# A two-layer decoder trunk: the first blocks of each MLP's down weights loaded earlier, and two small groups of work reordered

## The reference

```python
D_MODEL, SEQ, DEPTH, D_FF = 1024, 512, 2, 4096

def squared_relu_mlp(h, w_up, w_down):
    a = jax.nn.relu(h @ w_up)
    return (a * a) @ w_down

for layer in range(DEPTH):
    g = norm_gains[layer]
    hn = rmsnorm(x, g[0])
    ...                       # mix = attention of this layer on hn
    x = x + rmsnorm(mix, g[1])
    hn = rmsnorm(x, g[2])
    x = x + rmsnorm(squared_relu_mlp(hn, w_mlp_up[layer], w_mlp_down[layer]), g[3])
```

## Time and profile before

| | before |
|---|---|
| median of three executions | 1149.12 us (1147.21 to 1149.67) |
| the profiled execution's own time | 1146.72 us |
| its span | 1144.9 us |
| PE busy | 1085.0 us, 95% |
| DVE busy | 743.2 us, 65% |
| ACT busy | 541.0 us, 47% |
| POOL busy | 192.9 us, 17% |
| mean granted TensorE clock | 0.98 of full |

### The profile page before, as it was taken

How to read it: one execution, slowest core, us unless ns; L and a number is a source line. 1 busy time by engine, 2 the same in 40 slices (tenths; PEclk the granted TensorE clock), 3 DMA queues, 4 the chain that set the end, 5 groups by cost and what they waited for, 6 DMA issues and landing times. The chain is left out here.

```text
span 1144.9 us, 14901 instructions
## 1 busy us (share of the span) xinstructions
PE 1085.0 (95%) x5433; PEld 870.5 (76%) x5433; DVE 743.2 (65%) x1284; ACT 541.0 (47%) x1014; POOL 192.9 (17%) x338
## 2 busy tenths in 40 slices
PE   7999999989999999999899788999989999999997
PEld 6776678968888888888677665668968888888885
DVE  4354544368688696687276986644458688697674
ACT  6376653335345444435354366653435345444432
POOL 1353620000000000005303268440000000000004
PEclk9999999989999999999999889999989999999999
DMA  7431404245545355513413314003245635554411
GB/s 224 93 74 38 111 1 108 60 97 123 111 104 115 78 109 111 110 38 65 107 42 74 74 38 110 2 1 84 60 97 123 135 79 106 110 110 109 90 23 74
DMA packets 50793, 97.84 MB, mean 85 GB/s; under 512 B 4448, under 2 KB 4640, under 8 KB 50720
## 3 DMA queue, kind: packets, MB, share of 16 engines
q1 hardware_dynamic: 50208, 96.78, 37.7%
q10 hardware_dynamic: 512, 0.11, 0.1%
HBM read 94.78 MB, written 2.10 MB: 85 GB/s over the span
## 5 line engine op out<-in xcount | busy, mean ns | idle before, releaser
L1909 PE MATMUL bank<-r_hi,w_hi 128*128 128x512 f32 (+1 forms) x456 | 177.5, 389 | 0.0
L1910 PE MATMUL bank<-r_hi,w_lo 128*128 128x512 f32 (+1 forms) x456 | 177.4, 389 | 0.0
L1911 PE MATMUL bank<-r_lo,w_hi 128*128 128x512 f32 (+1 forms) x456 | 177.4, 389 | 0.0
L1534 DVE TENSOR_TENSOR w_lo<-w_raw,w_hi 128x1024 fp32r<-128x1024 f32 x84 | 101.7, 1224 | 94.0 <-ACT w_hi L1082 93.9
L1082 ACT ACTIVATE w_hi<-w_raw 128x1024 fp32r<-128x1024 f32 x84 | 87.4, 1054 | 124.8 <-PE bank L1911 64.3
L2250 PE MATMUL bank<-w_hi,hid_hi 128*128 128x512 f32 x336 | 132.8, 395 | 11.3 <-DVE hid_b L1524 11.3
L2251 PE MATMUL bank<-w_lo,hid_hi 128*128 128x512 f32 x336 | 132.2, 393 | 0.0
L2252 PE MATMUL bank<-w_hi,hid_lo 128*128 128x512 f32 x336 | 132.1, 393 | 0.0
L1091 ACT ACTIVATE w_hi<-w_raw,gT 128x512 fp32r<-128x512 f32 x96 | 64.4, 715 | 112.5 <-DMA w_raw<-in_w_mlp_up 82.7
L776 POOL TENSOR_TENSOR acc<-acc,G 128x512 f32<-128x512 f32 x8 | 13.0, 1652 | 586.4 <-ACT waste L950 586.4
L1919 PE MATMUL bank<-w_hi,r_hi 128*128 128x512 f32 x240 | 102.2, 426 | 8.2 <-DVE w_lo L1313 6.5
(11 more groups left out here) (198 smaller groups left out, 2138.9 us busy)
## 6 DMA issues: line engine op xcount, KB each, us to landing
w_raw<-in_w_mlp_up SPq DMA_DIRECT2D x64, 512.0 KB, 6.4
w_raw<-in_w_mlp_down SPq DMA_DIRECT2D x64, 512.0 KB, 7.0
w_raw<-in_b_w_in SPq DMA_DIRECT2D x16, 512.0 KB, 6.3
w_raw<-in_a_w_in SPq DMA_DIRECT2D x8, 512.0 KB, 6.5
w_raw<-in_a_w_out SPq DMA_DIRECT2D x8, 512.0 KB, 5.8
w_raw<-in_b_w_out SPq DMA_DIRECT2D x8, 512.0 KB, 6.2
X<-in_x SPq DMA_DIRECT2D x4, 512.0 KB, 6.9
w_raw<-in_a_w_in SPq DMA_DIRECT2D x8, 256.0 KB, 7.7
```

The costliest lines, as they stand in the source:

```text
L1534: nc.vector.tensor_tensor(half_of(w_lo[:, u % 2, :], a), b_of(PRODUCTS[i][1], a), half_of(w_hi[:, u % 2, :], a).bitcast(f32), ALU.subtract ...
L1909: nc.tensor.matmul(bank, whi, xhi, start=start, stop=False)
L1910: nc.tensor.matmul(bank, wlo, xhi, start=False, stop=False)
L1911: return nc.tensor.matmul(bank, whi, xlo, start=False, stop=stop)
```

## The change

Three edits, made in the code that both layers share, so each happens twice. SP issues B12 and B11 ahead of the next quarter's first up unit, which leaves the wait for the squares of X behind them. ACT does the four squares of X ahead of the relus of tiles 0 to 3. DVE makes T3 and T1 of quarter 0 ahead of the squares of tiles 4 to 7 in place of behind them; in the later quarters these sums stay where they were. No instruction is added or taken away.

```diff
@@ load_mlp, SP
                 sp.wait_ge(x_new, 8 * (2 * layer + 1))
                 fetch_down(0, "B22")
-                sp.wait_ge(xs_done, 8 * layer + 8)
-                fetch_up(1, 0)
                 sp.wait_ge(*low_of(up_unit(layer, 0, 2)))
                 fetch_down(0, "B12")
                 sp.wait_ge(*low_of(up_unit(layer, 0, 3)))
                 fetch_down(0, "B11")
+                sp.wait_ge(xs_done, 8 * layer + 8)
+                fetch_up(1, 0)
                 load_gain(2 + 2 * layer)
@@ mlp, ACT
+                for j in range(NB):
+                    x_square(2 * layer + 1, j)
                 for t in range(4):
                     relu_tile(layer, 0, t)
                 a_highs(0, 0)
-                for j in range(NB):
-                    x_square(2 * layer + 1, j)
                 b_highs(0, 0)
                 for t in range(4, 8):
                     relu_tile(layer, 0, t)
@@ mlp, DVE
                     squared(layer, 0, t)
                 a_lows(0, 0)
                 s3_sum(layer, 0)
+                t3_sum(layer, 0)
                 b_lows(0, 0)
+                for a in range(2):
+                    weight_sum(layer, 0, "T1", a)
                 for t in range(4, 8):
                     squared(layer, 0, t)
                 for q in range(LAST):
                     n = q + 1
                     up_split(layer, n, 0, (0, 1))
-                    t3_sum(layer, q)
-                    for a in range(2):
-                        weight_sum(layer, q, "T1", a)
+                    if q:
+                        t3_sum(layer, q)
+                        for a in range(2):
+                            weight_sum(layer, q, "T1", a)
                     for a in range(2):
                         hidden_sum(layer, q, "S1", a)
                         hidden_sum(layer, q, "S2", a)
```

## The result

| | before | changed |
|---|---|---|
| median of the timed runs | 1148.37 us (4 runs, 1147.21 to 1149.67) | 1132.08 us (4 runs, 1130.20 to 1133.60) |
| ratio | | 0.9857, 95% interval 0.9837 to 0.9877 |
| the profiled execution: time, span | 1146.72, 1144.9 us | 1133.60, 1131.8 us |
| PE busy | 1085.0 us, 95% | 1083.1 us, 96% |

Of 1148.37 us the ratio makes 16.4 us (14.1 to 18.7); 15.8 were forecast, and 1133.0 us.

A forecast was written before the change was run, and what follows sets the result against it. PE, busy 95%, bounds the kernel, so only its idle or slow time can be won: 5.84 + 5.78 + 2.14 + 2.07 = 15.8 us. From 1149.12 that gives 1133.3; forecast 1133.0 us, range 1130 to 1137.5.

The forecast's parts named there:

- The stall and its cause: PE's first product in each MLP waits, 11.3 us in all; cause: SP issues B11 late, held by the squares of X.
- 11.6 idle and 4.2 slow clock: PE at both products: idle 5.84 and 5.78 us, then slow first matmuls at half clock, 2.14 and 2.07 us.
- The signs: In the changed kernel: SP issues from about 204, L1082 about 225, L1587 about 218, L1570 about 228.6; MLP gap about 596.4.
- B11's landing: First MLP's load of B11: taken as in at 215.5 us, at the latest 224.8, against 237.4 before.
- the late case: B11 lands only when all loads are in, at 224.8 us, still before PE frees its slot at about 225.1.
- ACT's edit at nothing: Moving ACT's four squares of X (4.7 us) costs nothing, covered by 8.6 us of ACT's own idle time.
- DVE's edit: T3 and T1 moved ahead cost nothing when B11 is early; 4.2 us left at the squares, 3.1 at the next up unit.
- (a): Rival: only idle time at the products returns, the 4.2 us of slow matmuls stay or reappear; 1137.5 us, chance 0.05.
- (b): Rival: DVE's moved sums come late, a new wait of up to 4.7 us per MLP; 1142.7 us, chance 0.05.
- (c): Rival: slower, T1 ahead of tile 4's square while B11 lands late, 2.35 us more per MLP; 1153.8 us, chance 0.03.
- (d): Rival: something else holds SP between 204 and 220 us, so no change; 1149 us, chance 0.02.
- the point where a stall begins: With T1 ahead of the squares, landing to product takes 6.55 us, so PE stalls if B11 lands after 229.2.

The follow-up runs named there:

- fill25: Kernel before plus 25 unread matmuls on PE ahead of each MLP's first product: 1144.58 us, 0.9981 of before.
- act_only: Kernel before with only ACT's squares of X moved ahead of the relus; SP and DVE as before: 1130.50 us, 0.9851 of before.
- dve_only: Kernel before with only DVE's T3 and T1 moved ahead of the squares of tiles 4 to 7: 1151.24 us, 1.0033 of before.
- fill12: Kernel before plus 12 unread matmuls on PE ahead of each MLP's first product: 1147.56 us, executed once.
- sp_act: Kernel before with SP's issue order and ACT's squares changed, without the DVE edit: 1130.51 us, 0.9847 of before.

## Why the prediction was right

**The stall and its cause.** Right. The last link named by the profile was a square on DVE, the cause two engines further back, SP's wait for the squares of X. With either cure, earlier issue or earlier squares, the wait was gone.

**The size.** 15.8 us forecast, 15.87 in the two MLPs, 16.4 (14.1 to 18.7) in the timed runs. The split into 11.6 idle and 4.2 slow clock is borne out by fill25: the two products became 4.15 us shorter there, though 0.8 of it was lost again at the next up units, which the changed kernel does not lose. The signs came too: SP issues B12 at 205.51, L1587 runs at 219.09, L1082 at 226.41, L1570 at 229.78, each about 1.3 us later than written, as this MLP starts 1.28 us later. Only the distance of the two products came out at 597.84 in place of 596.4, because the stage between the MLPs was 1.49 us longer.

**Where I chose.** For B11's landing I took 215.5, which is 216.8 with this MLP's later start. ACT's row can't show it, since ACT was waiting for PE, but the DMA list can: for B11's second issue alone, at 208.80, it gives 9.1 us to landing, so 217.9, 1.1 us later than taken and far from the late case. The issues behind it landed later: the next up unit's 10.5 and 13.2 us after 209.78 and 210.42, G 13.5 us after 211.08. So this trace shows these loads landing in the order of their issues, and what I had cited from the Trainium skill (DMA: Bandwidth & Descriptors, Queues, rings and completion order), that completion need not be in order, did not show itself. It decided nothing: either landing is before PE frees the slot.

**ACT's edit at nothing.** Right: relus of tiles 2 and 3 still waited 3.99 us for PE. But I took it for a part of the mechanism that merely cost nothing; act_only shows that it is a full cure by itself.

**DVE's edit.** I gave 4.2 us of room at the squares and 3.1 at the next up unit. Measured: tile 4 squared at about 232.7 for 237.03, 4.3 us; and the low part of the next unit's first row ends at about 239.2, for 237.03 + 5.45 = 242.5, 3.3 us. That this edit alone is a loss was right, with 3.8 us (2.3 to 5.3) where 4.7 were put.

**Rivals.** (a) refuted by the clock of the changed kernel and by fill25. (b) did not occur. (c)'s mechanism was shown real, at 6.47 us from landing to product, but B11 lands at 217.9, well before the point where a stall begins (229.2, here 230.5). (d) refuted by the issue rows.

**What I read too finely.** The forecast of 1133.0 leaned on the median of three runs; a fourth moved that median by 0.75 us, and in the later batches before stood at 1147.67 and 1146.75. The error of the forecast, 0.9 us, is of that size. The span's own forecast, 1129.1, missed by 2.7 us, all of it in stages that the change does not touch.

The Trainium skill's advice not to fit the warm-up to a count of slow matmuls (TensorE: Matmul & The Clock Gate, What's actually happening) does apply to the count: ten slow intervals behind each stall before, nine and 13 in dve_only, 13 in fill12. But the term as a whole was a quarter of this change's gain, so it should be in the sum with its spread.

## What to carry to other kernels

A wait that the profile puts down to a short operation is often the end of a chain: follow it back until a queue stands still for a reason that has nothing to do with the data. Where a load is held by another load's reason, it can be freed by reordering the queue or by meeting that reason earlier, and one of the two is enough; test each alone before keeping both. Work moved ahead of what TensorE waits for is free only as long as its input comes early: the same edit brought 0.2 us in each MLP or cost 7 us in all, depending on when the block landed.

## What the runs showed of the hardware

A stall of TensorE may cost more than its length. Behind waits of 5.6 to 7.8 us, of 3.98 and of 3.41 us the granted clock was 0.50 (1.2 GHz) and the next matmuls of 512 columns came every 0.427 us in place of 0.227; behind those of 2.99, 2.83, 0.96 and 0.82 us it stayed 1.00 (2.4 GHz). The length of the wait does not decide alone: in the attention stage of sp_act PE waited 2.57 us until 558.70, and the granted clock was 0.50 from 559 to 560. Matmuls whose results nobody reads, put into the gap, kept it at 1.00 and made the kernel 2.2 us (0.8 to 3.6) faster. And a profile's span alone can't judge a change of a few us in this kernel: stages with unchanged code differed by up to 3.9 us from profile to profile.
